# A hybrid-mixer layer and a sparse-attention layer in one program: c's sums ahead of the turned x, the mixers' constants in two groups, gate chunks in halves with a planned search order, attention's dense products in single pieces

## What is computed

```
shift, scale, gate = split(silu(c) @ ada_w + ada_b, 3)
h    = rmsnorm(x) * (1 + scale) + shift
proj = h @ w_in                       # attention, rwkv and gla inputs
x    = x + gate * rmsnorm(concat(attn, rwkv, gla) @ w_out)
# second layer
proj = rms_norm(x) @ w_in_2           # q, k, v, index q/k/w, z_a, u, z_b, gates
iscore = sum_h relu(qi_h . ki) * wi_h ; idx = top_256(iscore, allowed)
a = softmax(q . k[idx]) @ v[idx] * silu(z_a)
b = pooled(u) @ pool_w * silu(z_b)
y = sigmoid(g0) * (a @ w_branch_a) + sigmoid(g1) * (b @ w_branch_b)
x = x + y @ w_out_2
```

## Time and profile before

| | |
|---|---|
| median of 3 runs | 3898.22 us (3897.89 to 3898.88) |
| the profiled execution | 3894.62 us, its span 3892.9 us |
| mean granted TensorE clock | 0.981 of full speed |
| PE busy | 3661.4 us (94%) |
| DVE, ACT, POOL busy | 1822.9, 1591.5, 423.4 us (47%, 41%, 11%) |
| DMA | 282 MB, mean 72 GB/s |

### The profile page before, as it was taken

The page is one execution under the profiler, slowest core; times in us unless marked ns, Lnnn a source line. Parts: engine busy times, 40 slices in busy tenths (PEclk is TensorE's granted clock), DMA queues, the critical chain, the costliest instruction groups (busy, mean ns, idle before and its releaser), DMA issues. The chain is left out here.

```text
span 3892.9 us, 68948 instructions
## 1 busy us (share of the span) xinstructions
PE 3661.4 (94%) x28140; PEld 2737.0 (70%) x28140; DVE 1822.9 (47%) x4514; ACT 1591.5 (41%) x3591; POOL 423.4 (11%) x695
## 2 busy tenths in 40 slices
PE   5999999995999999989999999999978999999998
PEld 4888888874666666567777777777766666666676
DVE  3111111124777777433667678656683333333322
ACT  1222222222443434213556566877752333433320
POOL 0000000003445444210000000000000000000000
PEclk9999999997999999999999999999989999999999
DMA  8111111104112221231111114212115211111111
GB/s 281 51 50 50 50 50 50 47 36 170 65 71 83 90 73 71 82 124 45 46 50 48 49 62 144 73 53 68 53 40 176 74 44 60 51 43 41 65 62 57
DMA packets 137283, 282.13 MB, mean 72 GB/s; under 512 B 27416, under 2 KB 84648, under 8 KB 130480
## 3 DMA queue, kind: packets, MB, share of 16 engines
q1 hardware_dynamic: 130240, 268.90, 19.5%
q0 software_dynamic: 2304, 8.39, 0.5%
q10 hardware_dynamic: 4464, 1.02, 0.1%
HBM read 181.80 MB, written 96.47 MB: 71 GB/s over the span
## 5 line engine op out<-in xcount | busy, mean ns | idle before, releaser
L2430 ACT ACTIVATE at_pT<-at_bank 128x512 f32<-128x512 f32 (+3 forms) x320 | 154.9, 531 | 614.2 <-PE at_bank L2322 612.9
L275 PEld LDWEIGHTS p_bank<-p_hT,w_in 128*128 128x128 f32 x3328 | 375.4, 192 | 7.7 <-issue 7.7
L275 PE MATMUL p_bank<-p_hT,w_in 128*128 128x128 f32 x3328 | 376.8, 274 | 0.0
L1826 PEld LDWEIGHTS p_bank<-p_hT,w_in_rest 128*128 128x128 f32 x3072 | 351.8, 195 | 31.2 <-issue 17.0
L1826 PE MATMUL p_bank<-p_hT,w_in_rest 128*128 128x128 f32 x3072 | 358.2, 279 | 11.8 <-DVE p_st L2102 11.7
L2448 DVE CUSTOM_DVE_ANT_0 at_s<-at_bank,at_bias 128x512 f32<-128x512 f32 (+3 forms) x320 | 182.8, 609 | 387.4 <-PE at_bank L2309 384.1
L281 PE MATMUL p_bank<-w_in,p_hT 128*128 128x512 f32 (+2 forms) x1024 | 310.5, 461 | 0.0
L1947 ACT ACTIVATE p_r<-p_acc,p_mid 128x384 f32<-128x384 f32 (+13 forms) x224 | 292.6, 1306 | 30.7 <-DVE p_acc L2129 26.4
L281 PEld LDWEIGHTS p_bank<-w_in,p_hT 128*128 128x128 f32 x1024 | 171.9, 190 | 124.0 <-issue 118.2
L1010 PE MATMUL b_banks<-b_wout,b_yT 128*128 128x512 f32 x512 | 248.0, 610 | 3.7 <-DVE b_yT L1340 2.2
L1817 PE MATMUL p_bank<-arena,p_hT 128*128 128x512 f32 x512 | 232.8, 608 | 10.0 <-ACT arena L1963 8.6
(11 more groups left out here) (405 smaller groups left out, 5681.9 us busy)
## 6 DMA issues: line engine op xcount, KB each, us to landing
stage<-p_st SPq DMA_DIRECT2D x16, 1856.0 KB, 5.8
arena<-stage SPq DMA_DIRECT2D x16, 1856.0 KB, 7.6
at_rest<-stage SPq DMA_DIRECT2D x16, 1280.0 KB, 5.9
stage<-p_pr SPq DMA_DIRECT2D x128, 128.0 KB, 1.8
p_ada<-in_ada_w SPq DMA_DIRECT2D x4, 2048.0 KB, 15.1
p_xt<-in_x SPq DMA_DIRECT2D x16, 512.0 KB, 3.2
b_x<-in_x SPq DMA_DIRECT2D x16, 512.0 KB, 3.3
x<-b_x SPq DMA_DIRECT2D x16, 512.0 KB, 3.0
```

Of the source, the lines that this page charges most:

```text
L275: last = mm(out, w_in[:, k, c:c + P], hT[:, k, 1:P + 1], start=(k == 0), stop=(k == KD - 1))
L1826: last = mm(bank[:, m * P:(m + 1) * P], weights(k, c + m * P, c + (m + 1) * P), hTs[:, n % 2, k, :], start=(k == 0), stop=(k == KD - 1))
```

## The change

1. In first_projections the four loads that the LoRA mixing needs get a semaphore of their own (`lora_loaded`), a new semaphore `ones_ready` stands after POOL's memsets, and PE sums chunks 0 and 1 before `turn_x(1)` and before it waits for `setup_done`.
2. In mixers the tile load is split from the three `late` loads, five constants (`first_loaded`) are issued before those, and the wait for the other eleven moves to their first uses (POOL `lower_levels`, PE `start_inverse`, DVE `take_grams`). POOL runs `key`, `kk_length`, `bonus_terms`, then `level_distances`; ACT runs `decays(0)` before `level_exps(0)`; DVE runs `bonus(0)` after `scaled_vectors(0)`.
3. In projections a gate chunk is two steps, h = 0 and 1, of four products each; ACT and SP act at h = 1. `plan()` keeps a clock for each of PE, ACT and DVE, with a cost of its own for ACT and DVE in each H step (`search_cost`), and places search steps by how far ACT and DVE are behind PE.
4. In attention a dense product has eight pieces instead of four, and they are also placed between the turned blocks.

```diff
+                pool.sem_inc(S["ones_ready"], 1)
...
-                pool.wait_ge(S["weights_loaded"], N_WEIGHTS)
+                pool.wait_ge(S["lora_loaded"], 64)
...
-                pe.wait_ge(S["setup_done"], 1)
-                turn_x(1)
+                pe.wait_ge(S["ones_ready"], 1)
                 for c in range(4):
+                    if c == 2:
+                        turn_x(1)
                     pe.wait_ge(S["chunk_used"], c + 1)
...
+                pe.wait_ge(S["setup_done"], 1)
+                pe.wait_ge(S["weights_loaded"], N_WEIGHTS)
```

```diff
-                fetch(0)
-                for n, name in ((KK_, "rwkv_k_k"), (KA_, "rwkv_k_a"), (LNW, "rwkv_ln_w"), (LNB, "rwkv_ln_b")):
+                fetch_tile(0)
+                first(sums[:, :], A["k_tri"][:, 1, :])
+                first(chunk_of[:, :], A["k_chunk_of"])
+                for n, name in ((KK_, "rwkv_k_k"), (KA_, "rwkv_k_a")):
+                    first(rows[:, n, :], row(A[name][0:1, :]))
+                first(rows[:, RK_, :], row(A["rwkv_r_k"].rearrange("a h d -> a (h d)")))
+                fetch_late(0)
+                for n, name in ((LNW, "rwkv_ln_w"), (LNB, "rwkv_ln_b")):
...
-                pool.wait_ge(S["weights_loaded"], N_WEIGHTS)
+                pool.wait_ge(S["first_loaded"], N_FIRST)
...
-                level_distances(0)
                 key(0)
                 kk_length(0)
+                bonus_terms(0)
+                level_distances(0)
                 level_keys(0)
...
+                decays(0)
                 level_exps(0)
-                decays(0)
...
+                    dve.wait_ge(S["kn_ready"], n + 1)
                     tt(X4[:, 3, :], kn[:, :], ex[:, 2, :], ALU.mult).then_inc(S["X4_ready"], 1)
...
                 key_squares(0)
-                bonus(0)
                 sums_less(0)
                 scaled_vectors(0)
+                bonus(0)
```

```diff
+def search_cost(slot, step):
+    act = dve = 0.0
+    if slot.a is not None:
+        act = len(halvings(step, ACT_HALVINGS, SELECT_STEPS)) * (0.75 + 1.03e-3 * (slot.a + 1) * P)
+    if slot.b is not None:
+        w = (slot.b + 1) * P
+        if step < SELECT_STEPS - 2:
+            dve = len(halvings(step, HALVINGS - ACT_HALVINGS, SELECT_STEPS - 2)) * (0.62 + 1.17e-3 * w)
+        else:
+            dve = 1.0 + 4.65e-3 * w if step == SELECT_STEPS - 2 else 0.6 + 3.0e-3 * w
+    return act, dve
...
+        if kind == "D":
+            pe, done = pe + 3.6, (n, s)
+            act = max(act, pe) + act_work[s] if s in act_work else act
+            dve = max(dve, pe) + dve_work[s] if s in dve_work else dve
+        else:
+            pe = pe + 1.85
+            act = max(act, pe) + 0.5 if s else act
+        index_behind, act_behind, dve_behind = (1.5, 3.0, 6.0) if kind == "D" else (0.5, 3.0, 15.0)
...
-            if narrow > wide or not ready or (indexed and kind == "X"):
+            if not ready or dve > pe + dve_behind or act > pe + (index_behind if kind == "X" else act_behind) or (indexed and kind == "X"):
                 break
```

```diff
+                            if (g * nb + kb) % 2:
+                                yield
...
-                        if m % 2:
-                            yield
-                    last.then_inc(S["spare_done"], 1)
+                        if m == 3:
+                            last.then_inc(S["spare_done"], 1)
+                        yield
...
+                    left = 8
+                    for _piece in range(len(blocks(ORDER[(step + 1) // PAIRS_A])) - 2 if step + 1 < STEPS else 0):
+                        next(others, None)
+                        next(others, None)
+                        next(pieces, None)
+                        left -= 2
+                    if 0 <= step < STEPS:
+                        for _piece in range(left - len(blocks(ORDER[n]))):
+                            next(others, None)
+                        for _turned in turn_probabilities(step):
+                            next(others, None)
                     for _piece in others:
-                        next(pieces, None)
-                    for _piece in pieces:
                         pass
-                    if 0 <= step < STEPS:
-                        turn_probabilities(step)
```

More of the change, by code:

```diff
@@ L1572, in units_before, with halvings @@
     return sum(len(s.units) for s in SLOTS[:j])
+def halvings(step, count, steps):
+    return range(count * step // steps, count * (step + 1) // steps)
+def search_cost(slot, step):
[9 more added lines that the diff above has]
+    return act, dve
@@ L1585, in plan @@
-    order, wide, narrow, at = [], 0.0, 0.0, 0
-    done = (-1, 0)
+    dense += [("G", k, h) for k in range(PAIRS * GATE_CHUNKS) for h in range(2)]
+    search = [step for slot in SLOTS for step in [("X", slot.j, m) for m in range(len(slot.units))] + [("H", slot.j, e) for e in range(SELECT_STEPS)]]
+    act_work, dve_work = {0: 0.7, 1: 3.6, 3: 1.5, 4: 0.7}, {1: 1.8, 2: 5.6, 3: 4.8, 5: 4.7}
+    order, at, pe, act, dve, done = [], 0, 0.0, 0.0, 0.0, (-1, 0)
     for step in dense:
         order.append(step)
-        wide += 3.6
-        narrow += {"D": 1.5, "G": 0.4}[step[0]]
-        if step[0] == "D":
-            done = step[1:]
+        kind, n, s = step
+        if kind == "D":
[6 more added lines that the diff above has]
+        index_behind, act_behind, dve_behind = (1.5, 3.0, 6.0) if kind == "D" else (0.5, 3.0, 15.0)
@@ L1602, in plan @@
+            order.append(search[at])
             at += 1
-    return order + [step for step, cost in search[at:]]
+    return order + search[at:]
 PLAN = plan()
@@ L1904, in _ @@
                             pe.wait_ge(S[f"gate_w_loaded{m // 4}"], 16)
-                        bank = bank_for("gate", n)
+                        if s == 0:
+                            gate_bank = bank_for("gate", n)
                         c = GATE_COLUMNS[m // 4] + m % 4 * P
-                        for k in range(KD):
-                            last = mm(bank[:, 0:2 * P], weights(k, c, c + P), hTg[:, g % 2, k, :], start=(k == 0), stop=(k == KD - 1))
-                        last.then_inc(S["gate_done"], 1)
+                        for k in range(s * KD // 2, (s + 1) * KD // 2):
+                            last = mm(gate_bank[:, 0:2 * P], weights(k, c, c + P), hTg[:, g % 2, k, :], start=(k == 0), stop=(k == KD - 1))
+                        if s == 1:
+                            last.then_inc(S["gate_done"], 1)
                     if kind == "X":
@@ L2002, in _ @@
                             act.wait_ge(S["index_done"], n + 1)
-                        for k in range(ACT_HALVINGS * s // SELECT_STEPS, ACT_HALVINGS * (s + 1) // SELECT_STEPS):
+                        for k in halvings(s, ACT_HALVINGS, SELECT_STEPS):
                             halve(SLOTS[n], k)
@@ L2193, in _ @@
                             dve.wait_ge(S["act_halved"], n)
[L2194 removed]
                         if s < SELECT_STEPS - 2:
[L2196 removed]
+                            for k in halvings(s, HALVINGS - ACT_HALVINGS, SELECT_STEPS - 2):
                                 halve(SLOTS[n], ACT_HALVINGS + k)
```

79 lines of the change are left out of this document (46 added, 33 removed).

## The result

The changed kernel takes 3783.4 us (median of 4 runs, 3778.6 to 3785.4) against 3898.05 (4 runs, 3893.7 to 3898.9): a ratio of 0.9706, with a 95% interval of 0.9689 to 0.9723. The forecast was 3806, with a range of 3776 to 3838. One term, that of attention, was too small by 26; three of the other four were too large by up to 3.

What follows compares the result with a forecast made beforehand. PE, busy 94% of the span, bounds the kernel; its work stays, so gains come from its waits and clock. Gains of 15.9 + 13.5 + 22 + 25 + 16 = 92.4 us give 3802.2, or 3806 on the median's scale; range 3776 to 3838.

Steps and rivals of the forecast that it cites:

- Part 1: Program start: summing c's first chunks earlier lets the first product with h start at 43.8; gain 15.9 us, bounds 10 and 17.
- Part 2: Mixers' start: earlier constants (10 us sooner setup) and new order move the chain 13.5 us; bounds 8 and 15.5.
- Part 3a: Search inside projections: 44 us of waits and slow clock fall to 22; gain 22 us, bounds -5 and 35.
- Part 3b: End of projections: search ends earlier, so the gap before attention falls from 34.0 to 9; gain 25 us, bounds 15 and 29.
- Part 4: Attention: all 33.3 us of waits for ACT's copies go, 16.5 for denominators come; gain 16 us, bounds 8 and 33.
- The new wait: Attention: PE waits for DVE's denominators behind the output product's last piece, 1.1 us 15 times, 16.5 us.
- all 33.3 us of the earlier trace go: Attention: pieces after every two turned blocks give ACT's copies time, removing PE's whole 33.3 us wait for the turned probabilities.
- (a): Attention: the new wait for the denominators doesn't show, attention gives its whole 33; 3789 us, chance 0.13.
- (b): Projections: new stalls replace old ones (gain 0 instead of 22) or the search still ends behind the gates; 3828 us, chance 0.21.
- the four kinds of waits: PE's waits inside projections (ACT, DVE's take_mixed, queries, relus): 34.2 us before, 18 forecast to be left.
- (c): Attention: turned blocks mixed with pieces run at 1.2 instead of 2.4 GHz; slower, up to 4111 us, chance 0.04.
- the clock in attention is below 1: Attention: sign that the forecast is wrong; it expected the granted clock to stay 1.00.

## Why the prediction came out as it did

**Part 1** (15.9 forecast, 12.9 measured). The third chunk did start early (27.48, forecast 28.0) and the fourth followed at once behind it, but at 36.16 instead of 33. Two steps failed: "took 21.7 us each to land, so 27.9 and 30.0" and "the third keeps DVE busy to 33". The row's 21.7 is the time of the first load alone (6.21 + 21.7 = 27.9, where the third chunk starts); the profile has no landing for the second, which came near 34.8 by the wait in the run with the mixing moved away. And POOL's mixing, freed by the same change, now fell beside DVE's chunk and stretched it by 3.6 us. Without POOL the load holds the chunk; the two hide one another.

**Part 2** (13.5, measured 13.1 over the stretch). The two halves were each a little off: the constants brought 7.8 us instead of 10, as POOL, released by the last of the five, began its setup 17.8 us behind the end of the stage before, where 16.1 was forecast; the order brought 2.9 instead of 3.5. The forecast that ACT's level exponentials would hold up the copies was right in kind (PE's wait of 2.29 for them). The Gram products came 10.7 us closer to the stage's start (41.7 to 31.0), not 13.5; the further 2.4 us lie within what this stretch varies by (776.7 here, 779.8 in another execution of the same kernel). So the mechanism is right, but the closeness of 13.1 to 13.5 is luck.

**Part 3a** (22, measured 19.2). The waits went from 34.2 to 17.0 as forecast (18 left), kind by kind: `take_mixed` 7.2 for 7, relus 6.1 for 7, queries 3.7 for 2.1, the silu none for 2. The rest is the clock behind the stalls, put at 6 and measured as 19.2 - 17.2 = 2. In two other executions of the same order the stretch took 1205.2 and 1204.9 instead of 1208.6, with waits of 16.5 and 16.2, which makes this rest 5; so it is 2 to 5, and the whole term 19 to 23.

**Part 3b** (25, measured 26.3). The gap is 7.7 for a forecast 9. DVE ended its selection at 2843.28 + 2.29 = 2845.6, 4.7 us ahead of PE's last gate at 2850.3 (forecast: about 4), since ACT's last halving ended 45.8 us ahead of it (forecast: 45).

**Part 4** (16, measured 41.9, outside its bounds of 8 to 33). The new wait was right within a microsecond (15.6 for 16.5). The step that failed is "all 33.3 us of the earlier trace rows go": the mechanism was right and the size was not. The stalls that went had cost 65.9 us, because 0.17 us of each stood in the busy column and the short ones had no row. Some 6.5 of the 32.6 that this adds to the 33.3 went again in what the forecast had too small on the other side (18.8 for 16.5, 5.2 for 1), which leaves the 26. The upper bound was taken from the same row and failed with it. The forecast had the means to see it: in the timeline, eight unstalled matmuls take 0.87 us from start to start, and eight with a stall behind them 1.35.

**The rivals.** (a) did not come: the denominators are waited for. (b) did not: the four kinds of waits halved. (c) did not: from 3000 to 3700 us, with pieces and turned blocks mixed, the granted clock was 1.00, as in the kernel that has the turned blocks in one run. The forecast's sign for it, "the clock in attention is below 1", did show, as 0.99 over the stage, but for something else. The clock was 0.53 of full speed in the stage's first 8 us, behind the gap, and 0.68 over 5 us near its end. The kernel with the pieces ahead of the turned blocks has both (0.55 and 0.68), so the mixing is not the reason. The later one in the changed kernel, and in that one (columns as in the earlier trace rows):

```profile
3741.00:3746.00 5.00, 5.00 (x31) 4.65 (x31) 1.38 (x2) 0.27 (x1) 0.31 (x1) 0.68 0.28 108
```

```profile
3784.00:3789.00 5.00, 5.00 (x30) 4.59 (x30) 1.38 (x2) 0.27 (x1) 0.43 (x1) 0.68 0.28 108
```

By the rule of the Trainium skill (page "TensorE: Matmul & The Clock Gate", Part 4) the clock might have fallen; with ordinary products between the turned blocks the trace shows none of it.

## What to carry to other kernels

In these profiles the idle time given for a wait of PE is a lower bound of what the wait costs, since a matmul's row runs on while the next could already start: price a stall by the distance between starts, stalled against unstalled, above all where there are many short ones, and take the upper bound of a gain from that and not from the idle row. An engine that a change sets free works at a new time, so look for whom it then runs beside: here POOL beside DVE. When a row gives one time for several loads, look at what waited for the last of them. In a written order of three engines keep the few places where a bank's release decides clear of long steps; that was worth 11 us more than the cost rule alone, while loosening its limits cost more than it gave.

## What the runs showed of the hardware

- DVE operations with two inputs beside POOL's tensor operations: six of 128x512 took 7.65 us for 4.06, and POOL's 1.54 for 1.04. In mixers the same: one multiplication of DVE (L1299, 128x256) took 2.29 us beside a POOL operation of 2.07 in the kernel with the old first tile; the like multiplication behind it took 0.43.
- A matmul's row in the profile (its end is modelled) ends 0.17 us behind the point at which a next one without a wait would start, for blocks of 128x128 (1.04 - 0.87 for eight).
